# A router and expert kernel: queue order of ScalarE and VectorE by a rule, one more load slot, and an earlier release of a PSUM bank

## The chip, the cores and the metric

The kernel runs on one core of a Trainium2 chip. The metric is the device time of one execution in microseconds. The kernel before took 681.7 us (median of three executions, 681.65 to 683.01).

## What is computed

1024 tokens of width 1024 pass one layer: RMSNorm, a causal pooling mixer, a residual add, RMSNorm, a two-level router that gives each token two of 32 experts, and the gated MLP of those experts, summed into the residual; then a last RMSNorm. What concerns this case is the expert stage.

```python
def expert_block(args):            # for each of the 32 experts
    xblk, e = args                 # its tokens, gathered
    g_part, up = jnp.split(xblk @ w_gu[e], 2, axis=-1)     # 1024 -> 2 x 512
    return (jax.nn.silu(g_part) * up) @ w_dn[e]            # 512 -> 1024
out = out.at[buf_tok].add(yb * buf_w[:, None])             # weighted, added per token
```

All is fp32. The kernel reaches the accuracy with pairs of rounded numbers: each fp32 operand is split into a high part (a copy to fp32r) and a low part (the operand minus the high part), and a product is three matmuls, high by high, low by high and high by low.

## The kernel before, in words

**Loads.** The 192 MB of expert weights come in 192 loads of 1 MB, here called pairs (two blocks of 128 rows, 128 x 2048 fp32 in a buffer), from SyncE's queue (L500). Six pairs belong to an expert: four of gate and up (GU_PAIRS), two of the down projection. They are counted through: `pair(s, j)` is 6s - 2 + j, so that step s begins with pair 6s - 2. Step s of TensorE is the four gate-up pairs of the s-th expert and then the two down pairs of the expert before. A load waits until the pair that last stood in its buffer has been used (`raw_free`), and until the load four before has landed (FLIGHT, L542).

**Splitting.** ScalarE copies a pair into a high buffer (`split_pair`, L883), VectorE writes the low part over the loaded buffer (`low_pair`, L1192), TensorE multiplies (L1698, 12 matmuls for a pair). There are 18 buffers for loads and 3 for high parts. From pair 22 on (step 4, HEAD) 3 of the 18 are given over to high parts (GIVEN), from step 22 (E - 10) another 2; ScalarE waits there (`hi_free`) for the pair that last had the high buffer.

**A step's other work.** TensorE transposes the gathered tokens of the next expert after the third gate-up pair (`turn_x`, into the banks XT); ScalarE and VectorE split them (`split_x_block`, `low_x`). When the gate-up sums stand (bank pair GU), ScalarE takes silu, VectorE multiplies (`hidden`, L1458), TensorE transposes the result behind the first down pair (`turn_h`, L1768), ScalarE and VectorE split it (`split_h_block` L969, `low_h` L1462). ScalarE evicts the down sums with the gate (`copy_y`, L979), GpSimd adds them into memory by an indirect DMA (L735).

**Small steps.** At steps 6, 9, ... 27 the expert has at most 64 tokens. High and low part of the tokens stand side by side as 128 columns, and a gate-up pair is 8 matmuls (L1710). The sums lie in two halves of the partitions: ScalarE copies the lower half out (`copy_lower`, L941), VectorE adds the halves into `lower` in SBUF (`add_lower`, L1444, semaphore `summed`), silu and product work from `lower` (L962, L1450). TensorE's first gate-up pair of the following step writes the same bank GU, and waits for the split tokens (`x_split`) and for the product (`hid_made`); `turn_h` of a small step comes behind that first pair. The tokens of a small step are transposed with one 128 x 128 and seven 64 x 64 transposes (L1750, L1752), others with eight of 128 x 128 (L1757).

**The order of each queue** is written out. Each engine has its own loop over the steps; before part j of step s ScalarE and VectorE both take up all pairs up to `pair(s, j) + LEAD[s]`. LEAD is 0 to step 4, then 1, 1, 1, 2, then 1, 1, 2 six times, then 1, 2, 3, 4, 4, 4. At j = 0 stand silu and the tokens, at j = 2 the split of h, and behind the pairs of j = 2 the eviction of y.

## Time and profile before

| | kernel before |
|---|---|
| median of the runs | 681.7 us |
| profiled execution: time / span on the core | 681.78 / 680.0 us |
| TensorE busy (matmul records) | 637.3 us, 94% |
| VectorE busy | 606.2 us, 89% |
| ScalarE busy | 529.6 us, 78% |
| GpSimd busy | 258.8 us, 38% |
| moved by DMA | 242.83 MB |
| granted clock, mean | 0.992 |

The span is what the traces show from the first to the last instruction; 1.8 us of the execution's time lie around it. Steps 1 to 31 lie between about 101 and 658 us. Matmul records overlap, so that a stretch in which TensorE is "busy" throughout says only that it did not wait; times of starts are the better measure.

### The profile page before, as it was taken

To read this page: it belongs to the slowest core of one execution; us is meant where nothing else is said; L and a number is where in the kernel's file an instruction comes from. 1 tells how busy PE (TensorE), PEld (TensorE's weight loads), DVE (VectorE), ACT (ScalarE), POOL (GpSimd) and SP (SyncE) were. 2 spreads that over 40 slices of the span, in tenths; PEclk is the share of its full clock that TensorE was granted. 3 is DMA by queue.
4 is the path that set the end of the run, shared out by engine and by line. 5 is a ranking of instruction groups with operands and counts; after the bars stand their busy time and mean duration, and the time that the engine had idled before them with its cause. 6 is when DMAs were issued, how large, how long until landed. Compare 5 with 4: busy or idle time off the path is not lost.

```text
span 680.0 us, 9755 instructions
## 1 busy us (share of the span) xinstructions
PE 637.3 (94%) x3524; PEld 534.9 (79%) x3524; DVE 606.2 (89%) x497; ACT 529.6 (78%) x454; POOL 258.8 (38%) x211
## 2 busy tenths in 40 slices
PE   6899989999999999999899999999999999989993
PEld 4899978888887787788788778778778778778872
DVE  6986789988898997998998998998998998999977
ACT  5996526777878977976977887896896896898794
POOL 5000020054444544564444354353354354352531
PEclk9999989999999999999999999999999999999997
DMA  8997869997999999999999999997999999999496
GB/s 291 420 419 249 274 195 421 358 360 235 375 354 374 403 397 365 387 406 367 385 400 381 389 392 390 387 389 278 376 405 384 383 404 389 399 384 371 158 352 238
DMA packets 44148, 242.83 MB, mean 357 GB/s; under 512 B 8695, under 2 KB 9855, under 8 KB 19522
## 3 DMA queue, kind: packets, MB, share of 16 engines
q1 hardware_dynamic: 34322, 220.39, 82.5%
q0 software_dynamic: 9776, 21.79, 11.8%
q8 instruction: 29, 0.48, 0.3%
q14 instruction: 21, 0.17, 0.1%
HBM read 228.24 MB, written 27.26 MB: 376 GB/s over the span
## 4 chain that ended last, share of the span: by engine, by line
PE 54%; DVE 22%; ACT 13%; issue 6%; DMA 4%; ACTq 0%; POOL 0%; SPq 0%; POOLq 0%; DVEq 0%
PE psum L1698 40%; DVE w_lo L1192 14%; ACT w_hi L883 7%; PE psum L1626 3%; ACT ysb L979 2%; PE psum L1768 2%; DMA total<-ysb,dst_now 2%; PE psum L1612 2%; ACT w_lo L883 2%; PE psum L1644 2%; DVE lower L1444 1%; DVE x_lo L1428 1%; PE psum L1752 1%; PE psum L1710 1%; PE psum L1757 1%
## 5 line engine op out<-in xcount | busy, mean ns | idle before, releaser
L1192 DVE TENSOR_TENSOR w_lo<-raw,w_hi 128x2048 fp32r<-128x2048 f32 x98 | 221.7, 2289 | 19.6 <-ACT w_hi L883 19.3
L1192 DVE TENSOR_TENSOR w_lo<-raw,w_lo 128x2048 fp32r<-128x2048 f32 x94 | 211.8, 2285 | 12.7 <-ACT w_lo L883 11.6
L883 ACT ACTIVATE w_hi<-raw 128x2048 fp32r<-128x2048 f32 x98 | 184.9, 1914 | 6.6 <-PE psum L1698 6.6
L1698 PE MATMUL psum<-w_lo,x_hi 128*128 128x512 f32 x620 | 174.2, 393 | 11.0 <-DVE x_lo L1428 11.0
L883 ACT ACTIVATE w_lo<-raw 128x2048 fp32r<-128x2048 f32 x94 | 175.9, 1913 | 0.0
L735 POOL DMA_INDIRECT total<-ysb,dst_now x29 | 63.2, 2180 | 214.7 <-ACT ysb L979 214.7
L1698 PEld LDWEIGHTS psum<-w_lo,x_hi 128*128 128x128 f32 x620 | 114.9, 188 | 37.9 <-DVE x_lo L1428 14.1
L1698 PE MATMUL psum<-w_lo,h_hi 128*128 128x512 f32 x312 | 92.3, 392 | 0.5 <-DVE h_lo L1462 0.5
L698 POOL DMA_INDIRECT xg<-normed,src_now x29 | 64.5, 2223 | 22.3 <-POOL src_now L706 22.3
L1698 PE MATMUL psum<-w_lo,x_lo 128*128 128x512 f32 x236 | 72.9, 390 | 0.0
L1698 PEld LDWEIGHTS psum<-w_lo,h_hi 128*128 128x128 f32 x312 | 58.3, 188 | 13.1 <-DVE h_lo L1462 0.9
L1698 PE MATMUL psum<-w_hi,h_hi 128*128 128x512 f32 x200 | 63.5, 399 | 0.0
L1698 PE MATMUL psum<-w_hi,h_lo 128*128 128x512 f32 x200 | 61.7, 390 | 0.0
L1710 PE MATMUL psum<-w_lo,x_hi 128*128 128x512 f32 x212 | 53.2, 390 | 0.0
L731 POOL COPY dst_now<-src_all 128x1 int32<-128x1 int32 x29 | 32.8, 1132 | 52.8 <-DMA total<-ysb,dst_now 52.8
L1698 PEld LDWEIGHTS psum<-w_lo,x_lo 128*128 128x128 f32 x236 | 44.3, 188 | 9.4
L706 POOL COPY src_now<-src_all 128x1 int32<-128x1 int32 x29 | 50.9, 1757 | 1.7 <-PE psum L1757 1.7
L969 ACT ACTIVATE h_hi<-psum 128x512 fp32r<-128x512 f32 x32 | 19.1, 597 | 37.7 <-PE psum L1698 29.1
L1698 PE MATMUL psum<-w_hi,x_hi 128*128 128x512 f32 x148 | 48.0, 405 | 0.0
L956 ACT ACTIVATE silu<-psum 128x512 f32<-128x512 f32 x24 | 14.3, 597 | 41.8 <-PE psum L1698 41.8
L1710 PEld LDWEIGHTS psum<-w_lo,x_hi 128*128 128x128 f32 x212 | 39.7, 188 | 8.3
L1698 PE MATMUL psum<-w_hi,x_lo 128*128 128x512 f32 x148 | 45.8, 391 | 0.0
(210 smaller groups left out, 945.8 us busy)
## 6 DMA issues: line engine op xcount, KB each, us to landing
raw<-in_expert_w_gu SPq DMA_DIRECT2D x128, 1024.0 KB, 8.5
raw<-in_expert_w_down SPq DMA_DIRECT2D x64, 1024.0 KB, 9.1
res<-in_x SPq DMA_DIRECT2D x8, 512.0 KB, 9.6
normed<-nx POOLq DMA_DIRECT2D x8, 512.0 KB, 7.5
total<-res SPq DMA_DIRECT2D x8, 512.0 KB, 9.0
raw<-total SPq DMA_DIRECT2D x8, 512.0 KB, 10.0
out<-raw SPq DMA_DIRECT2D x8, 512.0 KB, 4.3
pw_in<-in_pool_w SPq DMA_DIRECT2D x1, 1024.0 KB, 8.0
```

What stands on the lines that cost most here:

```text
L698: pool.indirect_dma_start(out=xg[0:slots, g, :], out_offset=None, in_=normed[:, :], in_offset=bass.IndirectOffsetOnAxis(ap=rows[0:slots].b ...
L706: nc.gpsimd.tensor_copy(src_now[:, g:g + 1], rows).then_inc(idx_now, 1)
L731: nc.gpsimd.tensor_copy(dst_now[:], src_all[:, col]).then_inc(idx_now, 1)
L735: pool.indirect_dma_start(out=total[:, :], out_offset=bass.IndirectOffsetOnAxis(ap=dst_now[0:slots].bitcast(u32), axis=0), in_=ysb[0:slots ...
L883: nc.scalar.activation(hi_at(s0, j), raw[q][:], ACT.Copy).then_inc(hi_done, 1)
L956: nc.scalar.activation(silu[:], gu[:, 0:F], ACT.Silu).then_inc(silu_done, 1)
L969: nc.scalar.activation(hi[:].rearrange("p k t -> p (k t)"), turned, ACT.Copy)\
L979: nc.scalar.activation(ysb[:], y, ACT.Identity, scale=gate_now[:]).then_inc(y_copied, 1)
L1192: V.tensor_tensor(w_lo[q][:], raw[q][:], hi_at(s0, j).bitcast(f32), ALU.subtract)\
L1626: last = mm(PY[:, g * 2 * P:(g + 1) * 2 * P], a[:, c, :], b[:, c, :], start=(n == 0), stop=(n == len(terms) - 1))
L1698: last = mm(dst[:, n * N:(n + 1) * N], a[:, ch, :], b[:, c * D + n * N:c * D + (n + 1) * N], start=(ch == 0 and a is hi and b is b_hi), st ...
L1710: last = mm(dst[:, n * N:(n + 1) * N], parts_of[:, ch, :], b[:, c * D + n * N:c * D + (n + 1) * N], start=(ch == 0 and b is b_hi), stop=(c ...
```

## The change

ScalarE's and VectorE's loops are rewritten from step 4 on; steps 0 to 3 keep their order. A rule takes LEAD's place: `start(s)` is the first pair of step s, `lead(s)` is 2 up to step 28 and then 3, 4, 4, 4. ScalarE has split all pairs below start + lead before it waits for a step's gate-up sums, VectorE all pairs below start + lead - 1. Behind silu and the tokens come two more pairs, then the split of h, then at once the eviction of y, and the rest of the pairs. After a small step one of the two pairs stands between `low_x` and the product (VectorE) and between `split_x_block` and silu (ScalarE). At step 31 ScalarE splits all that is left before the eviction, which waits for the indirect DMAs. GIVEN takes two load buffers at step 4 in place of three: 5 high buffers and 16 for loads, from step 22 on 7 and 14. TensorE's first gate-up pair after a small step waits for `summed` in place of `hid_made`. Small steps are transposed as the others are; the 64 columns that matter are read from the layout of the 128.

```diff
-    GIVEN = {HEAD: 3, E - 10: 2}
+    GIVEN = {HEAD: 2, E - 10: 2}
     SPARE = sum(GIVEN.values())
-    LEAD = [0] * 5 + [1, 1, 1, 2] + [1, 1, 2] * 6 + [1, 2, 3, 4, 4, 4]
...
+        def start(s):
+
+            return s * PER_STEP - (PER_STEP - GU_PAIRS)
+
+        def lead(s):
+
+            return min(4, 2 + max(0, s - (E - LATE - 1)))
...
+        def up_to(following, one, s, n):
+
+            while following[0] < min(start(s) + n, MAIN):
+                one(*place(following[0]))
+                following[0] += 1
...   ScalarE, both split_x_block and low_x
-                    nc.scalar.activation(x_hi[:, :, 0:H], XT[:, 0:KD * H].rearrange("p (k t) -> p k t", k=KD),
+                    nc.scalar.activation(x_hi[:, :, 0:H], XT.rearrange("p (k t) -> p k t", k=KD)[:, :, 0:H],
...   ScalarE
+            def step(s, s0, turn):
+                if s < FREE_STEP:
+                    early_step(s)
+                    return
+                n = lead(s)
+                up_to(split_next, split_pair, s, n)
+                if s == E:
+
+                    act.wait_ge(pair_used, end_free[TILES // 2])
+                    for i in range(3):
+                        final_square(i, 0)
+                    nc.scalar.activation(warm[:, 1:2], eps[:], ACT.Silu)
+                if is_small(s - 1):
+
+                    copy_lower(s - 1, start(s - 1) + GU_PAIRS)
+                    split_x_block(s)
+                    up_to(split_next, split_pair, s, n + 1)
+                    silu_of_sums(s - 1, small_turn(s - 1, 0))
+                else:
+                    silu_block(s - 1, start(s - 1) + GU_PAIRS)
+                    if s < E:
+                        split_x_block(s, is_small(s))
+                up_to(split_next, split_pair, s, n + 2)
+                if s == E:
+                    final_square(3, 0)
+                    split_h_block(s - 1, end_free[TILES // 2], hi=h2_hi)
+                else:
+                    split_h_block(s - 1, start(s))
+                if s < E - 1:
+                    copy_y(s - 1, start(s), s - 2)
+                if s == E - 1:
+
+                    up_to(split_next, split_pair, s, 2 * PER_STEP)
+                    act.wait_ge(pair_used, start(s))
+                    act.wait_ge(pos_made, 1)
+                    act.wait_ge(y_stored, 16 * (E - LATE))
...   VectorE
+                n = lead(s) - 1
+                up_to(low_next, low_pair, s, n)
...
+                if is_small(s - 1):
+                    add_lower(small_turn(s - 1, 0))
+                    low_x(s)
+                    up_to(low_next, low_pair, s, n + 1)
+                    hidden_of_sums(s - 1)
+                else:
+                    hidden(s - 1)
+                    if s < E:
+                        low_x(s, is_small(s))
+                up_to(low_next, low_pair, s, n + 2)
...
+                else:
+                    low_h(s - 1)
...   TensorE
-            def turn_x(s, g, landed, few=False):
+            def turn_x(s, g, landed):
...
-                if few:
-                    nc.tensor.transpose(XT[:, 0:P], every(xg[:, g, :], KD, 0), ident[:])
-                    for c in range(1, KD):
-                        last = nc.tensor.transpose(XT[:, c * H:(c + 1) * H],
-                                                   every(xg[0:H, g, :], KD, c), ident[0:H, 0:H])
-                    last.then_inc(x_turned, 1)
-                    return
...
                     pe.wait_ge(x_split, s + 1)
-                    if not (isinstance(s, int) and s == 1):
+                    if isinstance(s, int) and is_small(s - 1):
+                        pe.wait_ge(summed, small_turn(s - 1, 0) + 1)
+                    elif not (isinstance(s, int) and s == 1):
                         pe.wait_ge(hid_made, s)
```

## Rows read from the trace of the kernel before

**Rows 1.** Waits from 120 to 620 us: who waits for whom, us, times, longest.
```profile
PE psum L1698 <- DVE x_lo L1428: 11.0, 8, 1.4
PE psum L1768 <- DVE hid L1458: 7.7, 8, 2.1
DVE w_lo L1192 <- ACT w_hi L883: 18.7, 34, 1.1
DVE w_lo L1192 <- ACT w_lo L883: 11.6, 21, 1.1
```

**Rows 2.** TensorE's timeline (start us, us, line), steps 3 and 4, then steps 13 to 16.
```profile
157.91 1.05 PE L1757 MATMUL psum<-ident,xg 128*128 128x128 f32 x8
175.80 1.05 PE L1757 MATMUL psum<-ident,xg 128*128 128x128 f32 x8
...
324.25 1.16 PE L1698 MATMUL psum<-w_lo,x_hi 128*128 128x512 f32 x4 [1.38 <-DVE x_lo L1428]
...
361.79 5.61 PE L1710 MATMUL psum<-w_lo,x_hi 128*128 128x512 f32 x24
...
376.95 1.16 PE L1698 MATMUL psum<-w_lo,x_hi 128*128 128x512 f32 x4 [1.38 <-DVE x_lo L1428]
```

**Rows 3.** VectorE's timeline at the end of small step 15.
```profile
371.71 2.28 DVE L1192 TENSOR_TENSOR w_lo<-raw,w_lo 128x2048 fp32r<-128x2048 f32 x1
373.91 1.21 DVE L1444 TENSOR_TENSOR lower<-psum,lower 64x1024 f32<-64x1024 f32 x1
375.05 1.20 DVE L1428 TENSOR_TENSOR x_lo<-psum,x_hi 128x1024 fp32r<-128x1024 f32 x1
376.18 0.67 DVE L1450 TENSOR_TENSOR hid<-silu,lower 64x512 f32<-64x512 f32 x1
```

**Rows 4.** ScalarE's timeline at the same place.
```profile
368.95 1.92 ACT L883 ACTIVATE w_lo<-raw 128x2048 fp32r<-128x2048 f32 x1
...
375.15 0.63 ACT L962 ACTIVATE silu<-lower 64x512 f32<-64x512 f32 x1 [2.17 <-DVE lower L1444]
```

**Rows 5.** Stretches of 17 us; last columns granted clock, DMA share, GB/s.
```profile
144.00:161.00 17.00, 17.00 (x82) 14.09 (x81) 15.24 (x10) 14.02 (x10) 8.06 (x8) 1.00 0.75 262
280.00:297.00 17.00, 16.21 (x78) 13.30 (x77) 16.71 (x10) 16.54 (x13) 9.44 (x7) 1.00 1.02 403
450.00:467.00 17.00, 17.00 (x81) 14.05 (x80) 16.37 (x10) 11.05 (x8) 7.18 (x5) 1.00 0.87 338
467.00:484.00 17.00, 15.62 (x73) 12.80 (x72) 13.52 (x9) 14.32 (x11) 7.13 (x5) 1.00 0.92 308
```

**Rows 6.** Two weight loads one after the other: issue, and us from issue to landing.
```profile
L500 SPq DMA_DIRECT2D raw<-in_expert_w_gu x1: 337/337/337, 356.2 to 356.2; - x1
DMA to landing us min/median/max: 7.4/7.4/7.4
...
L500 SPq DMA_DIRECT2D raw<-in_expert_w_gu x1: 333/333/333, 359.2 to 359.2; - x1
DMA to landing us min/median/max: 6.9/6.9/6.9
```

**Rows 7.** The load of pair 187 in the same form, then ScalarE's splits up to it.
```profile
L500 SPq DMA_DIRECT2D raw<-in_expert_w_gu x1: 331/331/331, 616.9 to 616.9; - x1
DMA to landing us min/median/max: 6.5/6.5/6.5
...
632.41 3.74 ACT L883 ACTIVATE w_lo<-raw 128x2048 fp32r<-128x2048 f32 x2
638.33 0.60 ACT L956 ACTIVATE silu<-psum 128x512 f32<-128x512 f32 x1 [2.18 <-PE psum L1698]
```

**Rows 8.** TensorE's two late waits for the product: steps 28 and 31.
```profile
605.17 0.75 PE L1768 MATMUL psum<-ident,hid 128*128 128x128 f32 x4 [2.13 <-DVE hid L1458]
659.40 0.75 PE L1768 MATMUL psum<-ident,hid 128*128 128x128 f32 x4 [1.54 <-DVE hid L1458]
```

**Rows 9.** From the chain that ended last: start us, us, what.
```profile
631.60 14.34 DMA total<-ysb,dst_now
```

More of the change, by code:

```diff
@@ L979, in copy_y, with early_step @@
                 nc.scalar.activation(ysb[:], y, ACT.Identity, scale=gate_now[:]).then_inc(y_copied, 1)
-            def step(s, s0, turn):
-                js = parts(s0)
-                for j in js:
-                    if s0 == 0 and j == 0:
+            def early_step(s):
+                for j in parts(s):
+                    if s == 0 and j == 0 or s == 1 and j < GU_PAIRS:
                         continue
-                    if s0 == 1 and j < GU_PAIRS:
-                        continue
-                    if s0 == E and j == hidden_at(s0):
-                        act.wait_ge(pair_used, end_free[TILES // 2])
-                        for i in range(3):
-                            final_square(i, 0)
-                        nc.scalar.activation(warm[:, 1:2], eps[:], ACT.Silu)
-                    if s0 > 1 and j == hidden_at(s0) and is_small(s0 - 1):
-                        copy_lower(s - 1, pair(s - 1, GU_PAIRS - 1) + 1)
-                        split_x_block(s)
-                        silu_of_sums(s - 1, small_turn(s0 - 1, turn))
-                    elif s0 > 1 and j == hidden_at(s0):
-                        silu_block(s - 1, pair(s - 1, GU_PAIRS - 1) + 1)
-                        if 1 < s0 < E:
-                            split_x_block(s, is_small(s0))
-                    if s0 == 0 and j == 2:
@@ L1016, in step @@
-                    if s0 == E and j == h_split_at(s0):
-                        final_square(3, 0)
-                        split_h_block(s - 1, end_free[TILES // 2], hi=h2_hi)
-                    elif s0 >= 1 and j == h_split_at(s0):
-                        split_h_block(s - 1, None if s0 == 1 else pair(s - 1, PER_STEP - 1) + 1)
-                    if s0 < FREE_STEP:
-                        split_pair(s, s0, j, turn)
-                    else:
-                        while split_next[0] <= min(pair(s, j) + ahead(s), MAIN - 1):
-                            split_pair(*place(split_next[0]))
-                            split_next[0] += 1
@@ L1027, in step @@
-                    if 2 <= s0 < E - 1 and j == h_split_at(s0):
-                        copy_y(s - 1, pair(s - 1, PER_STEP - 1) + 1, None if s0 == 2 else s - 2)
-                    if s0 == 0 and j == GU_PAIRS - 1:
+                    if s >= 1 and j == h_split_at(s):
+                        split_h_block(s - 1, None if s == 1 else pair(s - 1, PER_STEP - 1) + 1)
+                    split_pair(s, s, j)
+                    if s >= 2 and j == h_split_at(s):
+                        copy_y(s - 1, pair(s - 1, PER_STEP - 1) + 1, None if s == 2 else s - 2)
@@ L1030, in step @@
+                    if s == 0 and j == GU_PAIRS - 1:
                         split_x_block(1)
@@ L1464, in low_h, with early_step @@
                     .then_inc(h_split, 1)
[L1466 to L1469 removed]
+            def early_step(s):
+                for j in parts(s):
+                    if s == 0 and j == 0 or s == 1 and j < GU_PAIRS:
                         continue
[L1471 to L1485 removed]
+                    if s > 1 and j == 0:
+                        hidden(s - 1)
+                        low_x(s)
+                    if s == 0 and j == 1:
                         sort_experts()
@@ L1516, in step @@
                         low_pair(1, 1, 3)
+            def step(s, s0, turn):
+                if s < FREE_STEP:
+                    early_step(s)
+                    return
+                n = lead(s) - 1
+                up_to(low_next, low_pair, s, n)
+                if s == E:
+                    up_to(low_next, low_pair, s, PER_STEP)
+                    dve.wait_ge(nfin_in, 16)
+                    for i in range(3):
+                        final_norm(i, 0)
+                if is_small(s - 1):
[4 more added lines that the diff above has]
+                else:
+                    hidden(s - 1)
+                    if s < E:
+                        low_x(s, is_small(s))
+                up_to(low_next, low_pair, s, n + 2)
+                if s == E:
+                    late_add_copied()
+                    final_norm(3, 0)
+                    low_h(s - 1, hi=h2_hi, lo=h2_lo)
+                else:
+                    low_h(s - 1)
             def final_norm(i, turn):
```

65 lines of the change are left out of this document (16 added, 49 removed).

## The prediction

> **What bounds the kernel now.** I began with the waits of the expert stage and asked only who holds TensorE up. It never waits there for a weight pair; it waits eight times for the split tokens and eight times for the product [rows 1]. Next I took step lengths from the starts on TensorE's timeline. The transposes of steps 3 and 4 begin 17.89 us apart [rows 2], and no wait stands between them: this is a normal step at full pace, with 72 matmuls, one turn of x and one of h. A small step is 16 matmuls shorter; 24 of them take 5.61 us, so one takes (5.61 - 0.39)/23 = 0.227 us, 0.39 being the length of a single record, and 16 take 3.6. Three steps, one of them small, would take 3 x 17.89 - 3.6 = 50.0 us without a wait. The restarts after small steps 12 and 15 lie 376.95 - 324.25 = 52.70 us apart [rows 2]. So 2.7 us of each such period are waits of TensorE, about 1.5 for the tokens and the rest for the product.
>
> The third view was the queues in front of those waits. After a small step VectorE ends a low part, adds the halves, makes the low tokens and the product one right behind the other [rows 3]; TensorE goes on at 376.95, 0.1 us after the product's end at 376.85, although the tokens were ready at 376.25. VectorE is late there because it lost time before: 55 times it waited for a high part, 30.3 us in all [rows 1], since both engines go equally far ahead and each wait of ScalarE passes on to VectorE. The fourth view was DMA. Its share is 1.02 in an ordinary stretch [rows 5], and two loads issued 3.0 us apart land at 363.6 and 366.1, 2.5 apart [rows 6], so the engines are backlogged while SyncE still waits for buffers. Yet data are early: pair 187 lands at 623.4 and is split from about 634.3 on, as the second of two [rows 7]. TensorE sets the pace now, DMA is right behind it.
>
> **The change part by part.** *Bank free with the sums.* TensorE's restart after a small step waits for x_split and summed. Both are there 0.6 us before the product (376.25 against 376.85) [rows 3]. Alone this is 8 x 0.6 = 4.8 us. What is queued behind it is turn_h, one pair of 12 matmuls (2.7 us) later. The product now has a low part in front: 2.2 + 0.67 = 2.9 us after the tokens, so at worst TensorE waits 0.2 us at turn_h if the tokens were late, nothing if they were early.
>
> *ScalarE two ahead, VectorE one.* VectorE's own order hardly changes: before, it too stood one pair ahead at most waits and two ahead at small steps. What changes is that the high part that it wants is already there. I followed one period with a TensorE that never waits, 0 being the restart after a small step. A pair is 2.73 us (a normal step less 1.5 us for its turns, by six), so the second normal step ends at 18.4 + 17.9 = 36.3 (the first is half a microsecond longer, having two turns of h). Only then may h be split: 0.2 us of signal, ScalarE 0.6, VectorE 0.7, ready by 37.8. Four low parts at 2.2 us (373.91 - 371.71) take VectorE to 46.6, when ScalarE, which idles 2.17 us hereabouts today [rows 4], has the lower half out. The addition and the low tokens take 1.14 and 1.20 [rows 3]: tokens ready at 49.0, wanted at 50.0. A reserve of 1 us stands where 1.5 was lost. The product of the first normal step: its sums stand at 12.4, silu and product make it 14.1, or 14.3 behind VectorE's four low parts; wanted, one down pair later, at 15.2. That of the second: sums at 30.3, product 31.9, wanted 33.1, and VectorE idles 2 us before it, which absorbs an earlier delay. So I take all 2.7 us of a period. Bounds: nothing of it, if a delay eats the reserves at each turn, and 2.7. Seven periods and the first restart (1.4): 7 x 2.7 + 1.4 = 20.3 us. The wait of step 28, 2.13 us [rows 8], is the same kind and goes too, from a lead of two on VectorE. That of step 31, 1.54, comes from squares of the last norm ahead of silu; I leave it. Sum for TensorE: 22.4 us.
>
> *Five high buffers for six.* A split now waits for the pair five before. The last split ahead of silu then waits for the third gate-up pair, and takes 1.9 us [rows 4]; until the fourth pair ends, TensorE has the turn of x, 1.0 us, and 2.7 us of matmuls (1.8 in a small step). It is covered by 0.9 us or more. Without that cover silu would be up to 1.9 us late.
>
> *h and y.* The split of h stays after four pairs of ScalarE where it was after three or four; h is wanted some 9 us later. The eviction of y is one pair, 1.8 us, earlier, so that the indirect DMAs behind it on GpSimd start earlier, by themselves worth nothing until the end. There it shortens the way to the DMA of 14.34 us [rows 9] whose landing lets the last loads go. At step 31 the eviction moves behind two splits; it waited for that landing anyhow.
>
> *Whole transposes.* Eight of 128 x 128 take 1.05 us; the small form is bounded by the same number of instructions, eight, and what a column saves there is under 0.1 us of a 50 us period. I take 0; the ends are -1 and +1 us for eight steps.
>
> *One more load buffer.* Nobody waits for data now, so it gives nothing by itself, but it puts each load one pair earlier. In the stretches after steps 4 and 22, where buffers are given away, DMA ran at a share of 0.75, 0.87 and 0.92 [rows 5]: 17 x (0.25 + 0.13 + 0.08) = 7.8 us idle. One buffer more recovers about one load, 2.5 us, of the first, and at step 22, where loads will lag behind the buffers, most of the other 3.6: together some 5.5 us.
>
> **What is late next.** DMA must now move the same bytes in 50.0 us in place of 52.7. If it is at its limit, as the 2.5 us spacing says, the landed reserve pays. Pair 187 must be split before silu of step 30: landed 623.4, while a split begun at 638.33 - 1.9 = 636.4 would still be in time. That is 13.0 us; with the 5.5 recovered and 1.4 us that the product has at turn_h (2.7 less silu 0.6 and product 0.7), 19.9 us. TensorE could come 22.4 us earlier, DMA lets it come about 20, and the last loads and indirect DMAs, which now run closer to the end of the weights, cost something too: the indirect DMA took 14.34 us with little beside it [rows 9], and it will now run beside the last weights, of which each load is worth 2.5 us. I take half a load, 1.2 us, as an estimate. That leaves 18.8 us: 681.8 - 18.8 = 663.0 for the profiled execution, and since that stands within 0.1 us of the median, 663 for it too.
>
> The Trainium skill (DMA: Bandwidth & Descriptors, Where 436 GB/s comes from) puts the share of one core at about 358 GB/s, binding for loads from HBM, and a ceiling of 435 on the fabric. By the first figure no step could be shortened, and the trace does not agree with it: 403 GB/s in one stretch of 17 us. By the second a load of 1 MB would take 2.4 us, by estimate, and the trace is near that with 2.5.
>
> **The rivals.** *TensorE alone* (24%): DMA has more than I think, because part of the 7.7 us per period beyond 18 x 2.5 us overlaps; then 681.8 - 22.4 = 659.4. For it speaks that TensorE never waits for data, against it the spacing of 2.5 us.
>
> *Hand-overs stay* (16%): VectorE's delays of 0.1 to 0.3 us at each wait add up to the reserve of 1 us, and only the bank (4.8) and a quarter of the other 15.5 come, 8.7 us: 673, or 676 with little more than the bank.
>
> *Nothing of it arrives* (8%): the two pairs ahead don't free VectorE, because ScalarE's own waits are for TensorE's sums and its order was never what VectorE lacked; the bank's 4.8 us are given back at turn_h. Then the time stays: 681. The change doesn't do what it says in this case. Against it stand the 30.3 us [rows 1].
>
> *Slower* (10%): too few high buffers. The place is the split ahead of silu. If ScalarE comes to it more than 1.8 us after the third pair's end, because a split of four in a row waited for its buffer, silu, product and turn_h of that step are late. It decides once the cover of 0.9 us is gone, and wins over the gain only if it takes more than 0.8 us in each of 28 steps. A full late turn like that of 1.0 us in 28 steps costs 28 and gives back 20: 690. Against it: the pairs are used one after the other, so a delay of ScalarE does not grow.
>
> My forecast has the other 42%.
>
> **How the numbers follow.** Predicted 663. The range takes in TensorE alone with the transposes' -1 and a little of step 31 (658), and the hand-overs to their slower end (676). It leaves out the last two rivals, 18%. 0.2% is 1.4 us, about what a measurement of this kernel can tell from none. Faster: 42 + 24 + 16 = 82%. Of the third rival's 8%, 6 are within 0.2% and 2 slower; with the last rival slower has 12%.
>
> **What would show it.** In the profile after: the restart after a small step without a wait on x_lo, or under 0.3 us; restarts about 50 us apart at first; VectorE's waits for high parts under 10 us in place of 30.3; turn_h waits gone between steps 7 and 27; the first waits of ScalarE for a load after step 25, and in them the 2 us that TensorE doesn't get; DMA near 405 GB/s. Wrong would be: periods still above 52 us; ScalarE waiting for pair_used ahead of a split right before silu; loads in the waits before step 20.

## The result, and the profile after

The changed kernel takes 665.3 us (median of four executions, 664.71 to 666.33) beside 681.7 (681.25 to 683.01) for the kernel before in the same session: a ratio of 0.976, interval 0.974 to 0.978, faster by 16.4 us. The forecast was 663, with a range of 658 to 676. The profiled execution took 665.68 us and its span is 663.7. These are the busy shares, and TensorE's granted clock in 40 slices, from the page of the kernel after:

```profile
PE 634.7 (96%) x3524; PEld 538.4 (81%) x3524; DVE 602.8 (91%) x497; ACT 531.1 (80%) x454; POOL 298.6 (45%) x211
...
PEclk9999989999999999999999999999999999997997
```

The busy times stand nearly where they stood, since the same work is done; it is pushed together. Two things catch the eye. GpSimd is busy for 298.6 us, 40 more than before with the same instructions, so something holds its operations up. And the granted clock has a slice of 0.7 near 600 us.

**Where the time went.** This is TensorE's timeline, kernel after: starts of the eight transposes of a step's tokens (L1772), called the turn of the tokens. First the two turns of small steps at the ends of one period, then that of the last small step and one of the last steps.

```profile
293.30 1.05 PE L1772 MATMUL psum<-ident,xg 128*128 128x128 f32 x8
...
342.95 1.05 PE L1772 MATMUL psum<-ident,xg 128*128 128x128 f32 x8
...
541.56 1.05 PE L1772 MATMUL psum<-ident,xg 128*128 128x128 f32 x8
...
594.72 1.05 PE L1772 MATMUL psum<-ident,xg 128*128 128x128 f32 x8
```

A period of three steps is 342.95 - 293.30 = 49.65 us; before it was 52.70 [rows 2]. Set against the same turns of the kernel before, the gain can be followed:

| turn of the tokens | before | after | after is earlier by |
|---|---|---|---|
| first small step | 193.72 | 193.99 | -0.3 |
| second small step | 246.45 | 243.64 | 2.8 |
| last small step | 562.65 | 541.56 | 21.1 |
| two steps on | 596.52 | 574.96 | 21.6 |
| three steps on | 616.70 | 594.72 | 22.0 |
| four steps on | 634.50 | 619.42 | 15.1 |
| TensorE's last matmul starts | 668.58 | 652.24 | 16.3 |

Seven periods give 7 x 3.05 = 21.4 us. Then 6.9 us are lost in a single step, between 594.72 and 619.42. The waits of the kernel after, 120 to 620 us (engine, operation and line <- what it waited for: us, times, longest), show both halves:

```profile
PE psum L1783 <- DVE hid L1472: 7.7, 4, 4.0
DVE w_lo L1206 <- ACT w_hi L887: 7.0, 7, 4.2
...
ACT ysb L983 <- POOL gate_now L719: 5.3, 1, 5.3
...
DVE w_lo L1206 <- issue: 4.2, 1, 4.2
```

TensorE waits for tokens no more (11.0 us in eight times before [rows 1]), and VectorE waits for a high part 7.0 us in place of 30.3 [rows 1]. The 4.2 us under "issue" are a wait for a high part too, by the times: that low part starts at 595.64, and the split that it needs runs from 593.71 to 595.61 on ScalarE. So it is 11.2 us in all, of which two waits near the end, of 4.2 us each, are 8.4. TensorE is left with four waits for the product, one of 0.84 us at 164.72 and three near the end (the number in brackets is the wait):

```profile
549.31 0.75 PE L1783 MATMUL psum<-ident,hid 128*128 128x128 f32 x4 [1.23 <-DVE hid L1472]
...
583.19 0.75 PE L1783 MATMUL psum<-ident,hid 128*128 128x128 f32 x4 [1.71 <-DVE hid L1472]
...
605.19 1.13 PE L1783 MATMUL psum<-ident,hid 128*128 128x128 f32 x4 [3.95 <-DVE hid L1472]
```

Behind the last of them the clock falls. Kernel after, by stretch (busy us of each engine, then granted clock, DMA share, GB/s):

```profile
604.00:606.00 2.00, 0.81 (x5) 0.81 (x5) 2.00 (x3) 2.00 (x3) 0.58 (x1) 0.60 0.97 410
606.00:608.00 2.00, 2.00 (x7) 1.61 (x6) 2.00 (x2) 1.81 (x2) 0.00 (x0) 0.50 1.03 414
608.00:610.00 2.00, 2.00 (x7) 1.51 (x6) 2.00 (x2) 0.00 (x0) 0.00 (x0) 0.50 1.02 389
```

TensorE stood still for 3.95 us, and after that the granted clock is 0.50, the lower level of 1.2 GHz, until 610 and still 0.69 in the stretch from there to 612. Twelve matmuls there take about 5.3 us instead of 2.7. So the wait and the lower clock cost this step 3.95 + 2.6 = 6.6 of its 6.9 us.

**Why the product is late there.** Three engines must be read together. GpSimd, kernel after (start, length, operation):

```profile
520.98 9.33 POOL L739 DMA_INDIRECT total<-ysb,dst_now  x1 [1.49 <-ACT ysb L983]
...
538.72 0.21 POOL L719 COPY gate_now<-gate_all 128x1 f32<-128x1 f32 x1
...
572.14 11.88 POOL L739 DMA_INDIRECT total<-ysb,dst_now  x1 [1.16 <-ACT ysb L983]
```

VectorE in the same stretch:

```profile
519.97 4.48 DVE L1206 TENSOR_TENSOR w_lo<-raw,w_hi 128x2048 fp32r<-128x2048 f32 x2
524.37 4.48 DVE L1206 TENSOR_TENSOR w_lo<-raw,w_lo 128x2048 fp32r<-128x2048 f32 x2
528.77 0.68 DVE L1472 TENSOR_TENSOR hid<-silu,psum 128x512 f32<-128x512 f32 x1
```

And ScalarE, at the two evictions that waited for GpSimd's copy of the gate:

```profile
539.01 1.12 ACT L983 ACTIVATE ysb<-psum,gate_now 128x1024 f32<-128x1024 f32 x1 [4.75 <-PE psum L1720]
...
592.69 1.12 ACT L983 ACTIVATE ysb<-psum,gate_now 128x1024 f32<-128x1024 f32 x1 [5.28 <-POOL gate_now L719]
```

The indirect DMA that begins at 520.98 ends at 530.31, with the run of four low parts over at 528.8; the one of 572.14 ends at 584.0, with a run of five over at 582.5. The others of this kernel take 1.5 to 3.7 us. GpSimd's next operations start late, the gate is copied at 538.72, and the eviction, due 4.75 us earlier, starts at 539.01 (the view puts this wait down to PE, but the copy ended 0.1 us before the start). Behind the eviction on ScalarE stand the splits, behind these VectorE's low parts (idle for 4.16 us until 595.64), and behind these the product that TensorE waits for at 605.19. That was my first theory of the loss: *a chain that begins on GpSimd*. Its rival was that *the loads* set the last steps, and that any other wait only fills the same time.

### The profile page after: what moved, and what is told of

Same layout as the page of the kernel before. It is cut to its first block, busy times and chain, and to the rows that moved or that the text cites. A ratio compares the mean times of both kernels' runs of the same rounds, so it can differ in the third digit from the quotient of the medians.

```text
span 663.7 us, 9755 instructions
## 1 busy us (share of the span) xinstructions
PE 634.7 (96%) x3524; PEld 538.4 (81%) x3524; DVE 602.8 (91%) x497; ACT 531.1 (80%) x454; POOL 298.6 (45%) x211
## 4 chain that ended last, share of the span: by engine, by line
PE 78%; DVE 13%; ACT 3%; issue 3%; DMA 2%; POOL 0%; SPq 0%; ACTq 0%; DVEq 0%; POOLq 0%
PE psum L1720 56%; DVE w_lo L1206 8%; PE psum L1732 8%; PE psum L1772 4%; PE psum L1648 3%; PE psum L1783 2%; PE psum L1666 2%; PE psum L1634 2%; DMA pw_in<-in_pool_w 1%; PE psum L1657 1%; DVE raw L1544 1%; PE psum L1674 1%; ACT end_junk L819 1%; DMA out<-raw 1%; ACT w_hi L887 1%
## 5 line engine op out<-in xcount | busy, mean ns | idle before, releaser
L1206 DVE TENSOR_TENSOR w_lo<-raw,w_hi 128x2048 fp32r<-128x2048 f32 x113 | 255.1, 2284 | 12.0 <-ACT w_hi L887 7.7
L887 ACT ACTIVATE w_hi<-raw 128x2048 fp32r<-128x2048 f32 x113 | 213.1, 1914 | 12.7 <-PE psum L1720 12.7
L1206 DVE TENSOR_TENSOR w_lo<-raw,w_lo 128x2048 fp32r<-128x2048 f32 x79 | 178.4, 2283 | 0.0
L1720 PEld LDWEIGHTS psum<-w_lo,x_hi 128*128 128x128 f32 x528 | 98.4, 188 | 20.1
L1720 PE MATMUL psum<-w_hi,x_hi 128*128 128x512 f32 x240 | 75.9, 398 | 0.0
L1720 PE MATMUL psum<-w_hi,x_lo 128*128 128x512 f32 x240 | 74.2, 390 | 0.0
L1720 PEld LDWEIGHTS psum<-w_hi,x_lo 128*128 128x128 f32 x240 | 45.0, 188 | 9.6
L1720 PEld LDWEIGHTS psum<-w_hi,x_hi 128*128 128x128 f32 x240 | 43.4, 189 | 8.5 <-issue 0.5
L1720 PE MATMUL psum<-w_lo,x_lo 128*128 128x512 f32 x144 | 44.5, 390 | 0.0
L719 POOL COPY gate_now<-gate_all 128x1 f32<-128x1 f32 x29 | 35.6, 1227 | 18.5 <-DVE gate_all L1332 18.5
```

Source lines behind the costliest of these rows:

```text
L719: nc.gpsimd.tensor_copy(gate_now[:], gate_all[:, col]).then_inc(gate_put, 1)
L887: nc.scalar.activation(hi_at(s0, j), raw[q][:], ACT.Copy).then_inc(hi_done, 1)
L1206: V.tensor_tensor(w_lo[q][:], raw[q][:], hi_at(s0, j).bitcast(f32), ALU.subtract)\
L1720: last = mm(dst[:, n * N:(n + 1) * N], a[:, ch, :], b[:, c * D + n * N:c * D + (n + 1) * N], start=(ch == 0 and a is hi and b is b_hi), st ...
```

## The experiments

Each kernel is the changed kernel with the edit shown, unless it is said to start from the kernel before. Ratios are to the kernel before, run beside it on the same chip (medians 681.1 to 681.5).

**1. The bank held until the product, all else as changed.**

```diff
-                    if isinstance(s, int) and is_small(s - 1):
-                        pe.wait_ge(summed, small_turn(s - 1, 0) + 1)
-                    elif not (isinstance(s, int) and s == 1):
+                    if not (isinstance(s, int) and s == 1):
                         pe.wait_ge(hid_made, s)
```

> The changed kernel with one part undone: TensorE's first gate-up pair after a small step waits for the product again, not for the sums. Theory (the order of the queues frees VectorE, and the early bank is what lets the low part stand in front of the product): the tokens are ready, but the product now comes a low part later. In the changed kernel TensorE restarts at about 366.1 and the product ends at 368.0, so each of eight restarts waits 1.9 us: 8 x 1.9 = 15 us, about 680 us. Rival (the bank is worth only its 0.6 us each, 4.8 us): 670. Second rival (it decides nothing): 665.

674.53 us (673.65 to 674.94), ratio 0.990, 0.988 to 0.992. Not 680: the bank is worth 9.3 us here, not 16. The reason is in the view of TensorE's waits, 120 to 620 us, kernel of this run:

```profile
PE psum L1720 <- issue: 14.4, 8, 2.1
PE psum L1783 <- DVE hid L1472: 2.0, 2, 1.2
```

Eight waits of about 1.8 us stand where the first pair after a small step waits for the product, which now has a low part in front of it. (The view has them under "issue"; what the edit put there is the wait for the product.) The period is 51.67 us (turns of small steps at 297.43 and 349.10), 2.02 more than after; eight times that is 16.2 us, as I expected. But this kernel has no 3.95 us wait at the end (2.0 us in two waits for the product), so the last steps give some 7 us back.

**2. The bank alone, from the kernel before.** The same lines the other way round.

> The kernel before with one thing alone: the first gate-up pair after a small step waits for the sums and not for the product. Theory: the tokens are ready 0.6 us before the product at each of eight restarts, so the restart wait falls by 0.6 and the time by 4.8 us, to 676.5. Rival (VectorE is the one that is late, and goes on at the same time, so that the next wait for the product grows by as much): 680 to 681.

677.58 us (677.12 to 677.76), ratio 0.994, 0.993 to 0.996: 3.9 us, about as expected. TensorE's waits for the tokens fall from 11.0 to 5.8 us in eight times, and the period to 52.16.

**3. ScalarE one ahead like VectorE.**

```diff
-                n = lead(s)
+                n = lead(s) - 1
                 up_to(split_next, split_pair, s, n)
```

> The changed kernel with ScalarE only one pair ahead at its waits, as VectorE is. Theory (VectorE's 30 us of waits for high parts came from the two being equally far ahead): these waits return, over 20 us of them, the reserve of 1 us at the restart and at the product is used up in most periods and the time is 671 to 676 us. Rival (the gain came from the bank and the extra load buffer): VectorE waits, but TensorE does not, 665 to 667.

685.41 us (684.48 to 686.54), ratio 1.0065, 1.005 to 1.008: slower than the kernel before, although the bank is free and the transposes are whole. I expected 671 to 676. Its waits, 120 to 620 us:

```profile
DVE w_lo L1206 <- ACT w_hi L887: 25.4, 25, 1.5
DVE w_lo L1206 <- ACT w_lo L887: 20.2, 16, 2.1
...
PE psum L1783 <- DVE hid L1472: 12.5, 9, 3.4
...
PE psum L1720 <- DVE x_lo L1442: 7.0, 8, 0.9
```

VectorE waits 45.6 us for high parts, more than before (30.3). Why more is argued and not shown: the product now has a low part in front, and that low part's high part is not there. The second pair ahead on ScalarE is what the new order stands on. Both engines two ahead was not run.

**4. The order alone:** bank held, three buffers given, small transposes.

```diff
-    GIVEN = {HEAD: 2, E - 10: 2}
+    GIVEN = {HEAD: 3, E - 10: 2}
...
-                    if isinstance(s, int) and is_small(s - 1):
-                        pe.wait_ge(summed, small_turn(s - 1, 0) + 1)
-                    elif not (isinstance(s, int) and s == 1):
+                    if not (isinstance(s, int) and s == 1):
                         pe.wait_ge(hid_made, s)
...
+                if few:
+                    nc.tensor.transpose(XT[:, 0:P], every(xg[:, g, :], KD, 0), ident[:])
+                    for c in range(1, KD):
+                        last = nc.tensor.transpose(XT[:, c * H:(c + 1) * H],
+                                                   every(xg[0:H, g, :], KD, c), ident[0:H, 0:H])
```

> The new order of the queues of ScalarE and VectorE alone: bank held until the product, three load buffers given away at step 4, small transposes, all as before. Theory by the pieces measured one at a time in the changed kernel (bank held +9.3 us, small transposes +2.1, three given away +1.3, against 665.3): 678, if they add up. Rival (the order carries the gain, the pieces only help it): under 672. Rival (the order without the early bank is worse than the old order, since the low part stands in front of the product): 681 or more.

677.34 us (675.50 to 677.72), ratio 0.993, 0.992 to 0.995: 4.1 us, period 52.06. TensorE's waits of about 1.8 us in front of the first pair are there again, 14.5 us in eight times: most of what the order wins, the held bank takes back.

**5. Small transposes back, all else as changed** (the last block of the diff above alone).

> The changed kernel with the small steps' transposes in the small form again, one of 128 x 128 and seven of 64 x 64. Theory: both forms are eight instructions of the same length, the time stays within 1 us of 665. Rival (the small form has a wait for issue of 0.2 us at each of eight): 2 us slower, 667.

667.37 us (667.23 to 668.99), ratio 0.980, 0.978 to 0.981: the whole transposes are worth 2.1 us, and the period is 50.0. TensorE's timeline of this kernel, then that of the kernel after, at the turn of the same small step:

```profile
295.42 0.27 PE L1772 MATMUL psum<-ident,xg 128*128 128x128 f32 x1
295.62 0.98 PE L1774 MATMUL psum<-ident,xg 64*128 64x64 f32 x7
296.53 0.72 PE L1720 MATMUL psum<-w_lo,x_hi 128*128 128x512 f32 x2
```

```profile
294.10 1.17 PE L1720 MATMUL psum<-w_lo,x_hi 128*128 128x512 f32 x4
```

From the turn's start to the next pair it is 296.53 - 295.42 = 1.11 us with the small form and 294.10 - 293.30 = 0.80 with the whole one: 0.31 us a turn, and 0.35 in the period.

**6. Three buffers given, as before** (first lines of the diff of 4 alone).

> The changed kernel with three load buffers given away at step 4 as before: 6 high buffers, 15 for loads. Theory (DMA is saturated, one buffer more is one load, some 2.5 us, of reserve; the last gate-up load has 7 us of reserve in the changed kernel, from landing at 614.3 to the latest start of its split): reserve falls to 4 us or so, the time stays at 665 to 667. Rival (loads are what sets the end): 2.5 to 3 us slower, 668. Rival (high buffers are short at 5): faster, 662 to 664.

666.57 us (665.26 to 667.05), ratio 0.978, 0.977 to 0.980, which is within the measurement's reach of the changed kernel's 0.976. What the trace shows all the same is the load queue coming into view: ScalarE waits for weights 11.3 us in 18 waits after 480 us, in the kernel after never.

**7. The eviction takes its gate from the table of all gates,** not from GpSimd's copy.

```diff
-                    copy_y(s - 1, start(s), s - 2)
+                    act.wait_ge(pair_used, start(s))
+                    act.wait_ge(pos_made, 1)
+                    act.wait_ge(y_stored, (s - 2) * 16)
+                    nc.scalar.activation(ysb[:], Y, ACT.Identity, scale=gate_all[:, s - 2:s - 1]).then_inc(y_copied, 1)
```

> The changed kernel, in which ScalarE takes the gate of an eviction out of the finished table from step 4 on and does not wait for GpSimd's copy of it. Theory (the late stall of 3.95 us at step 29, the 2.7 us of matmuls at the low clock behind it and the wait of 1.23 us at step 26 come from evictions that waited 5.3 and 4.8 us for that copy, with VectorE's low parts behind them): the 5.3 goes, the evictions wait at most for the indirect DMA before, and the time falls by 4 to 8 us, to 658 to 661. Rival (the loads hold ScalarE there in any case; splits up to pair 181 could not start before 597.4): 1 to 3 us, 662 to 664. Rival (the eviction then waits for the indirect DMA as long as it did for the copy): 665.

664.42 us (664.24 to 665.21), ratio 0.975, 0.974 to 0.977. The expected 658 to 661 didn't come. The eviction now waits for the landing of the indirect DMA itself, 7.8 us in two times, and ScalarE for loads 3.5 us in six. This is the second rival of the expectation: one wait for GpSimd's work stands in the place of another, 7.8 us where it was 5.3 + 4.8, so the chain is shortened and not cut.

**8. VectorE one ahead to the end,** no ramp at step 29.

```diff
-                n = lead(s) - 1
+                n = 1
                 up_to(low_next, low_pair, s, n)
```

> The changed kernel with VectorE one pair ahead at its waits to the end, where it goes to 2 and 3 in steps 29 to 31. Theory (the fifth low part in a row ahead of step 28's product makes the wait of 1.71 us at 583.19, and the run of five is what GpSimd's indirect DMA of 11.88 us lies beside): that wait goes, the indirect DMA is over one low part earlier, and with it part of the stall of 3.95: 2 to 5 us, 660 to 663. Rival (a late low part of the last pairs takes the place): 665 or slower.

Four executions of 667.09, 668.17, 663.49 and 668.72 us, ratio 0.978, 0.975 to 0.982: not faster, and too scattered for more. The wait of step 28 at TensorE (1.71) is gone, that of step 29 is 2.17 in place of 3.95 (at 603.90), and the indirect DMA of that place takes 9.7 us instead of 11.9. But the wait of step 31 is now 4.09 in place of 0.30 (at 644.41): silu of that step is done at 639.9, while VectorE is with low parts until 639.5 and then with three tiles of the final norm, and starts the product at 643.68.

**9. A breath for GpSimd: one memset of one column between two low parts.**

```diff
+                    while low_next[0] < goal:
+                        low_pair(*place(low_next[0]))
+                        low_next[0] += 1
+                        if low_next[0] < goal:
+                            V.memset(breather[:, breaths[0]:breaths[0] + 1], 0.0)
+                            breaths[0] += 1
```

> The changed kernel (665.3 us) with one more VectorE instruction, a memset of one column, between any two low parts that VectorE makes one after the other. Theory: in the changed kernel the scatter's indirect DMA on GpSimd takes 9.33 us (from 520.98) and 11.88 us (from 572.14) because VectorE runs four and five low parts (two SBUF inputs each) back to back there, and GpSimd's own SBUF access stands behind all of them; a pause between two of them lets it through. Then both fall to 2 to 5 us, the two evictions of y (4.75 and 5.28 us of wait) start with at most 1 us of wait, TensorE's waits of 1.23, 1.71 and 3.95 us near 549, 583 and 605 go down to under 2 in sum, and so does the half clock behind the last (2.6 us): 658 to 661 us. Rival: the long operations have another cause (their own descriptors, or the DMA queue at its full rate), they stay at 9 us or more, and the time stays at 665 to 666 (some 60 memsets, hidden). Second rival: they go, but the loads set the last steps then, 663 to 664.

664.43 us (662.82 to 666.01), ratio 0.975, 0.973 to 0.977. The indirect DMAs stayed as they were, 9.38 us from 521.39 and 11.96 from 572.63. VectorE's timeline of this run shows that the edit made no pause:

```profile
524.82 2.28 DVE L1207 TENSOR_TENSOR w_lo<-raw,w_lo 128x2048 fp32r<-128x2048 f32 x1
524.84 0.06 DVE L1546 MEMSET breather<- 128x1 f32 x1
527.04 2.28 DVE L1207 TENSOR_TENSOR w_lo<-raw,w_lo 128x2048 fp32r<-128x2048 f32 x1
```

The memset stands 0.02 us behind the start of a low part, runs beside it, and the next low part follows at its usual distance of 2.2 us. **9b.** With the edit of 7 beside it the same holds:

> Both edits together: the memset between two low parts, and ScalarE's eviction of y taking its gate from the table of all gates (alone: 664.4 us). With the first theory only what is left of the scatter's delay counts: 657 to 661 us, and the eviction waits for nothing. If the pauses do nothing, as gate_direct alone: 664.4.

664.54 us (663.67 to 665.31), ratio 0.974, 0.972 to 0.976.

**10. The eviction three pairs later on ScalarE.**

```diff
                 if s < E - 1:
+                    up_to(split_next, split_pair, s, n + 5)
                     copy_y(s - 1, start(s), s - 2)
```

> The changed kernel with the eviction of y moved on ScalarE: three more pairs of the running step are split before it, so that a late scatter holds up no split. Theory of the chain (late scatter, late eviction, late splits, late low parts, late hidden): the waits of TensorE near 549, 583 and 605 go without any change to the scatters, though these still take 9 and 12 us: 658 to 662 us. Rival: y's bank comes free three pairs later in every step, so the next step's products into it wait, and the gain is given back over all steps: 668 to 680 us with waits for it in each step. A store that starts later at the end is no cost, since the last two steps evict on another path.

663.21 us (662.86 to 664.17), ratio 0.973, 0.971 to 0.975: the best of all kernels here, all four executions below all four of the changed kernel (664.71 and more), by 2 us, though the two intervals still overlap. GpSimd and TensorE of this run:

```profile
520.26 8.57 POOL L719 COPY gate_now<-gate_all 128x1 f32<-128x1 f32 x1
```

```profile
530.13 0.70 PE L1721 MATMUL psum<-w_hi,h_hi 128*128 128x512 f32 x2 [2.57 <-issue]
...
639.09 0.75 PE L1784 MATMUL psum<-ident,hid 128*128 128x128 f32 x4 [2.14 <-DVE hid L1473]
```

The rival of this run named a real price: at 530.13 TensorE waits 2.57 us for the bank of y, whose eviction stands behind a gate copy that itself took 8.57 us and ended at 528.83, where the four low parts end (528.8). But it is paid once, not at each step. The waits at 549 and 605 are gone (besides the two shown there is one of 1.18 at 584.20), and with the latter the lower clock: the granted clock is 1.00 in each stretch from 600 to 640. ScalarE waits for loads 6.3 us in seven times after 480 us. TensorE's last matmul starts at 648.25, 4.0 us earlier than in the kernel after, but 12.8 us of span follow it in place of 11.5, so that part of the gain is lost behind the weights.

**11. A real pause:** ten memsets of one column behind the second low part of such a run, from step 25 on.

```diff
+                    done = 0
+                    while low_next[0] < goal:
+                        low_pair(*place(low_next[0]))
+                        low_next[0] += 1
+                        done += 1
+                        if done == 2 and s >= 25 and low_next[0] < goal:
+                            for i in range(10):
+                                V.memset(breather[:, i * 8 + s - 25:i * 8 + s - 24], 0.0)
```

> The changed kernel with one real pause on VectorE: from step 25 on ten memsets of one column (0.06 us each, some 0.6 us) stand behind the second of the low parts that follow h's low part. The single memset of 0.06 us did nothing: the next low part began 0.02 us after it. In the changed kernel a waiting GpSimd operation ends 0 to 1.2 us behind the first operation of VectorE that reads PSUM (0.6 to 1.2 us long), so a pause of 0.6 us must let it through if two SBUF inputs on VectorE are what holds it. Theory: the scatter at 521 ends near 525 and takes about 5 us instead of 9.33, that at 572 about 5 instead of 11.88; the eviction's waits of 4.75 and 5.28 us fall under 2, TensorE's waits near 549, 583 and 605 under 3 us in sum: 659 to 663 us. Rival: they have another cause, and the scatters stay at 9 and 12 us: 665 to 667 (the pauses' 0.6 us a step on VectorE).

664.58 us (664.04 to 666.34), ratio 0.975, 0.973 to 0.976. GpSimd and then VectorE of this run:

```profile
521.58 4.92 POOL L740 DMA_INDIRECT total<-ysb,dst_now  x1 [1.49 <-ACT ysb L984]
...
574.09 5.07 POOL L740 DMA_INDIRECT total<-ysb,dst_now  x1 [6.46 <-ACT ysb L984]
```

```profile
520.56 4.48 DVE L1207 TENSOR_TENSOR w_lo<-raw,w_hi 128x2048 fp32r<-128x2048 f32 x2
524.99 0.11 DVE L1549 MEMSET breather<- 128x1 f32 x7
525.10 2.29 DVE L1207 TENSOR_TENSOR w_lo<-raw,w_lo 128x2048 fp32r<-128x2048 f32 x1
```

Seven of the ten memsets fill 0.11 us and the other three run beside the next low part, so the pause is 0.11 us and not 0.6, yet the indirect DMA now ends at 526.5 instead of 530.3 and takes 4.92 us in place of 9.33; the second takes 5.07 in place of 11.88. That the run of low parts held GpSimd up is shown by this. But the time hardly moved, and TensorE's waits near the end did not go (0.69, 1.23, 2.27 and 3.49 us). ScalarE, 540 to 612 us, waits for something else now:

```profile
ACT w_lo L888 <- DMA raw<-in_expert_w_gu: 6.7, 8, 1.8
ACT w_hi L888 <- DMA raw<-in_expert_w_gu: 4.1, 6, 1.5
ACT w_lo L888 <- DMA raw<-in_expert_w_down: 1.7, 1, 1.7
ACT w_hi L888 <- DMA raw<-in_expert_w_down: 0.7, 1, 0.7
```

That is 13.2 us of waits for weights, none of which the kernel after shows. The worst of them and what follows from it, ScalarE and then TensorE of this run:

```profile
603.74 1.91 ACT L888 ACTIVATE w_lo<-raw 128x2048 fp32r<-128x2048 f32 x1 [1.82 <-DMA raw<-in_expert_w_gu]
605.56 0.58 ACT L961 ACTIVATE silu<-psum 128x512 f32<-128x512 f32 x1
```

```profile
606.91 0.75 PE L1794 MATMUL psum<-ident,hid 128*128 128x128 f32 x4 [3.49 <-DVE hid L1473]
```

The last split ahead of silu starts 1.82 us late for its load, silu stands behind it, and the product of that step is the one that TensorE waits 3.49 us for. So loads that are late can make this stall by themselves. But do they stand in the same place in the kernel after? SyncE's issue of pair 180 (the split before that last one) and its landing, kernel after, then this run:

```profile
L504 SPq DMA_DIRECT2D raw<-in_expert_w_gu x1: 328/328/328, 583.2 to 583.2; - x1
DMA to landing us min/median/max: 11.6/11.6/11.6
```

```profile
L505 SPq DMA_DIRECT2D raw<-in_expert_w_gu x1: 328/328/328, 590.0 to 590.0; - x1
DMA to landing us min/median/max: 10.0/10.0/10.0
```

In the kernel after pair 180 lands at 594.8, and ScalarE splits it only at about 599.1, behind the late eviction. Here it lands at 600.0. And the loads of this profiled execution were late before the pause could act: pair 150 lands at 511.0 against 507.0, and the first memset is at 524.99. So the waits for weights seen here are not what the pause uncovered in the kernel after; most of that lateness the edit didn't make. It is also the slowest of this kernel's four executions (666.34).

What stands is this. The first theory holds as a mechanism, and in the profiled execution of the kernel after it is what made the stall of 3.95 us: the data were there 4.3 us before they were split. The loads are close behind it (in the same trace pair 174 lands at 578.2 and is split at 578.4, before the late eviction), and they make the same stall when they are some 5 us later. Over four executions each, runs 7, 9 and 11 won 0.7 to 0.9 us, which can't be told from none; only moving the eviction (run 10) won 2. How much the loads hold in an average execution of the kernel after, these runs don't tell.

## Why the prediction was right, and where it was not

**The period.** I had 52.70 to 50.0 us. The kernel with all of the change but the whole transposes has exactly this period, 50.0 (run 5), and the change 49.65. The hand-made period, with a reserve of 1 us at the restart, was right: TensorE doesn't wait once between 168 and 541 us. The first restart was to give 1.4 us and gave 1.7: from the turn before it to the turn behind it are 16.85 us (209.03 to 225.88) in place of 18.52 (209.10 to 227.62). The seven periods of the table hold this restart and the six after it; the eighth restart won as much, but a wait of 1.23 us at 549.31 that my sum didn't have took most of it. Two turns behind the last small step the gain is 21.6 us where my sum had 20.3.

**The parts don't add up, and I had added them.** Priced alone, the bank was 4.8 us, measured 3.9 (run 2). The order alone gave 4.1 (run 4). By periods that is 52.70 to 52.16 and to 52.06, together 1.2 us, while both at once (with the load buffer's change) take 2.7. Each stands in the other's way: with the old order the product is early and the tokens late, with the new one the product comes one low part later and a bank that waits for it costs 1.8 us eight times. I had followed the period with all parts in it, which is why the sum came out; the 4.8 us of the bank, read as a part of its own, would have been wrong for what the bank is worth inside (9.3 us, run 1).

**VectorE's waits** for high parts were to fall from 30.3 us to under 10: they are 11.2 with the one that the view calls "issue", and 2.8 without the two behind the late evictions. So the sign failed by the end of the kernel and held in the periods. The step that called ScalarE's second pair the point of the change is borne out by run 3 more than I claimed: without it all gain goes and 4 us more.

**Steps 28 and 31.** The wait of 2.13 us at step 28 was to go; 1.71 is still there (583.19). The step that failed is "from a lead of two on VectorE": the ramp puts a fifth low part in front of that product, and without the ramp the wait is gone (run 8). At step 31 I left 1.54 us; 0.30 are left (at 643.08).

**Whole transposes** were taken at 0, between -1 and +1 us. They gave 2.1 (run 5), outside these ends. I had held that eight instructions bound both forms; seven 64 x 64 and one whole take 1.11 us to the next pair, eight whole ones 0.80. The kernel before could have told it, since both forms were on its timeline (one small turn starts at 193.72, the next pair at 194.83).

**One more load buffer:** 5.5 us of idle DMA recovered was meant as reserve, not as time. Run 6 bears this out, 1.3 us that can't be told from none.

**The ends.** I had TensorE 22.4 us earlier, of which DMA lets 19.9 come, less 1.2 for the indirect DMAs: 3.7 us of loss. (The sum wrote 18.8 for what is left, having rounded 19.9 to 20; it is 18.7.) TensorE did come 22.0 earlier, up to 594.72, and lost 5.6 by the end. That both numbers are near is in part luck. The 22.0 hold the transposes (8 x 0.31 = 2.5), which I had at 0, and are short of 1.23 and 1.71 us for waits that came or stayed against the sum. And of the loss I had put 2.5 us down to data that aren't there, while TensorE passed the 19.9 us and no split in the kernel after waits for a load. The estimate of 1.2 us was the weak term: what it should have held is a late indirect DMA on GpSimd behind VectorE's low parts, which made a stall of 3.95 us and 2.6 us of lower clock behind it, of which a part comes back later. I had foreseen ScalarE's first waits for a load after step 25. They are in the traces where a buffer less is left (run 6) or the chain is changed (runs 7, 10, 11), but for run 11 part of them is the execution's own. SyncE shows what paces the loads, kernel after, 120 to 620 us:

```profile
SPq L546 <- DMA raw<-in_expert_w_gu: 188.4, 92, 4.3
SPq L546 <- DMA raw<-in_expert_w_down: 112.8, 46, 4.5
SPq L504 <- PE psum L1720: 71.4, 32, 6.7
```

L546 is the wait for the landing of the load four before, L504 that for a used buffer. Before, it was the other way round: 311.6 us for a used buffer, 69.6 for a landing. DMA runs at 389 to 414 GB/s in the stretches shown, the 405 that I named. Its bound was not as hard as I put it: in run 10 TensorE's last matmul starts 20.3 us earlier than before (648.25 against 668.58), more than the 19.9 that the loads were to allow.

**What stays open.** I can't say how much of the last 4 us (663.2 of run 10 to the 659.4 of TensorE alone) the loads hold and how much the waits that take turns. One profiled execution of each kernel is little: the wait near 605 is 1.85 us in run 9 and 3.38 in 9b, though the indirect DMAs are as long as in the kernel after. A kernel with fewer bytes in the last steps, or with the later eviction and the pause together, would tell; neither was run. A rival was left out too: ScalarE's own ramp. At step 30 it goes four pairs ahead, so that silu of step 29 (602.71) stands behind the split of pair 181 (600.91), while TensorE is at pair 176. Run 8 took the ramp off VectorE alone.

## What to carry to other kernels

When three engines hand work on, look at how far ahead each stands when it waits. Here the leader one step further ahead than its follower was worth 20 us against both one ahead (665.3 against 685.4), since the follower then inherits few of the leader's waits; both two ahead was not tried. Price a change of order and the release that goes with it as one, in a period worked through with both in it, since alone each may be eaten by what the other leaves. And where the chain behind a stall is found, ask which second wait stands close behind it. Remove the first to see, and compare in both traces when the data landed: two executions can differ there for reasons that the edit has no part in.

## What the runs showed of the hardware

**A run of VectorE operations with two SBUF inputs holds GpSimd's operations up.** In the kernel after 9.33 and 11.88 us for an indirect DMA's issue, against 1.5 to 3.7 for its others; in run 10 8.57 for a copy of the gate, against at most 2.2 for its others; in run 11 4.92 and 5.07 for the two indirect DMAs, with a gap of 0.11 us of other instructions in the run. That it is the two inputs in SBUF, and not another trait of the low parts, no run here shows. In the Trainium skill, page SBUF — State Buffer, section SBUF: two separate sides, the pair of ports that the two share is an exclusive lock, taken also by a VectorE operation with two SBUF inputs against a GpSimd operation that reads SBUF, and the other waits for it. The trace agrees, and adds that GpSimd need not get in between two such operations: it waited through four and five low parts that follow each other without a pause, and single memsets of 0.06 us among them didn't let it in (run 9: 9.38 and 11.96 us). Why it gets through between other low parts (an indirect DMA of 3.74 us at 579.08 in run 10, in the middle of a run of five) no run here shows.

**Seven transposes of 64 x 64 are no cheaper than whole ones.** With one whole transpose in front they take 1.11 us against 0.80, 0.31 longer than eight of 128 x 128, by the starts of the next matmul. A part of it may be the change of size between instructions; that was not taken apart.

**Behind a wait of some microseconds TensorE's clock can be at its lower level, and the wait's length alone doesn't decide.** Granted 0.50 from about 606 to 610 behind the stall of 3.95 us in the kernel after, and 0.59 and 0.56 from 608 to 612 behind 3.49 us in run 11. The stall's real price in the kernel after was so 6.6 us and not 4. Behind a wait of 1.86 us in run 7 it fell as well, to 0.50 from 606 to 608. But it is 1.00 throughout behind the waits of 2.57, 1.18 and 2.14 us in run 10, and 1.00 from 600 to 640 in run 6, with a wait of 3.22 us at 606.63 in it.
